# mLSTM gate products on four groups of array columns, partial sums added at the end

## What is computed

```python
xa, za, ub, gb, zb, gates = jnp.split(h @ w_in, ...)
xc = silu(causal_depthwise_conv_3(xa, conv_a_w, conv_a_b))
q = blockdiag(xc, wq)                  # 256 blocks of 4 x 4
k = blockdiag(xc, wk)
v = blockdiag(xa, wv)
gif = concatenate([q, k, v], axis=-1) @ w_if + b_if      # 8 outputs for each position
ig, lf = gif[..., :4], log_sigmoid(gif[..., 4:])
ha = mlstm_chunkwise(q, k * dh ** -0.5, v, ig, lf)
```

## Time and profile before

| what | value |
|---|---|
| median of 3 runs | 3956.01 us |
| lowest, highest | 3952.72, 3957.66 us |
| span of the profiled execution | 3958.0 us |
| PE busy | 3700.5 us, 93% |
| DVE busy | 2176.2 us, 55% |
| POOL busy | 1150.1 us, 29% |
| ACT busy | 901.6 us, 23% |
| mean granted TensorE clock | 0.964 |
| L1295 (`gif`) | 64 records, 30.2 us busy, between 2734.5 and 2884.4 us |

### The profile page before, as it was taken

How to read it: one execution, slowest core, us unless ns; L and a number is a source line. 1 busy time by engine, 2 the same in 40 slices (tenths; PEclk the granted TensorE clock), 3 DMA queues, 4 the chain that set the end, 5 groups by cost and what they waited for, 6 DMA issues and landing times.

```text
span 3958.0 us, 44173 instructions
## 1 busy us (share of the span) xinstructions
PE 3700.5 (93%) x17330; PEld 3000.4 (76%) x17330; DVE 2176.2 (55%) x2115; ACT 901.6 (23%) x1003; POOL 1150.1 (29%) x505
## 2 busy tenths in 40 slices
PE   7778999998999999998999999998999799998997
PEld 5667878877787887776788888876678688877875
DVE  7698451275744663444421221254369988866646
ACT  3344121121122332201210000022322122224221
POOL 0000434333333222223343443442122111214432
PEclk9999999999999999999999999998999899999998
DMA  3234313352135654543111111123333455563421
GB/s 128 72 81 118 98 46 114 109 154 64 32 124 147 157 151 121 153 104 106 43 48 48 48 48 48 40 88 91 130 123 128 141 148 173 145 205 128 156 85 59
DMA packets 538866, 415.58 MB, mean 105 GB/s; under 512 B 33352, under 2 KB 496584, under 8 KB 538720
## 3 DMA queue, kind: packets, MB, share of 16 engines
q1 hardware_dynamic: 477168, 293.94, 26.9%
q10 hardware_dynamic: 61552, 119.65, 8.1%
HBM read 291.00 MB, written 120.16 MB: 104 GB/s over the span
## 4 chain that ended last, share of the span: by engine, by line
PE 76%; DVE 15%; DVEq 3%; ACT 2%; issue 2%; DMA 1%; SPq 0%; ACTq 0%; POOL 0%; POOLq 0%
PE proj_ps L444 65%; DVE WORK L1112 5%; DVE Hlo L591 1%; ACT stage L472 1%; PE mix_ps L1295 1%; PE mix_ps L2160 1%; PE mix_ps L2159 1%; DVE Hlo L593 1%; PE mix_ps L695 1%; DVEq L551 1%; PE mix_ps L1442 1%; DVE AUX L674 1%; PE proj_ps L1453 1%; DVE WORK L2560 0%; PE mix_ps L701 0%
## 5 line engine op out<-in xcount | busy, mean ns | idle before, releaser
L444 PE MATMUL proj_ps<-Hhi,w_hi 128*128 128x512 f32 x4144 | 1330.9, 403 | 110.7 <-DVE Hlo L591 58.9
L444 PE MATMUL proj_ps<-Hlo,w_hi 128*128 128x512 f32 x4144 | 1293.6, 394 | 0.0
L444 PE MATMUL proj_ps<-Hhi,w_lo 128*128 128x512 f32 x4144 | 1289.5, 393 | 0.0
L411 POOL TENSOR_TENSOR w_hi<-w_raw,zero_col 128x1024 fp32r<-128x1024 f32 (+2 forms) x225 | 429.1, 1907 | 2165.3 <-PE proj_ps L444 1662.1
L444 PEld LDWEIGHTS proj_ps<-Hhi,w_hi 128*128 128x128 f32 x4144 | 774.9, 191 | 309.5 <-issue 84.5
L444 PEld LDWEIGHTS proj_ps<-Hlo,w_hi 128*128 128x128 f32 x4144 | 787.7, 190 | 169.0
L444 PEld LDWEIGHTS proj_ps<-Hhi,w_lo 128*128 128x128 f32 x4144 | 786.8, 190 | 168.8
L414 POOL TENSOR_TENSOR w_lo<-w_raw,w_hi 128x1024 fp32r<-128x1024 f32 (+2 forms) x225 | 583.5, 2593 | 32.0
L1112 DVE SCALAR_TENSOR_TENSOR WORK<-WORK,param_cols 128x1024 f32<-128x1024 f32 x240 | 368.3, 1535 | 18.8
L401 POOL TENSOR_TENSOR w_lo<-w_raw,w_hi 128x1024 fp32r<-128x1024 f32 x48 | 135.4, 2820 | 559.4 <-ACT w_hi L395 559.4
L472 ACT ACTIVATE stage<-proj_ps 128x1024 f32<-128x1024 f32 x112 | 130.2, 1163 | 634.8 <-PE proj_ps L444 633.9
(11 more groups left out here) (421 smaller groups left out, 3614.7 us busy)
## 6 DMA issues: line engine op xcount, KB each, us to landing
w_raw<-in_w_in SPq DMA_DIRECT2D x101, 512.0 KB, 4.7
w_raw<-in_sgu_w_in SPq DMA_DIRECT2D x24, 512.0 KB, 3.8
w_raw<-in_w_out SPq DMA_DIRECT2D x24, 512.0 KB, 4.1
w_raw<-in_w_gate SPq DMA_DIRECT2D x22, 512.0 KB, 3.8
w_raw<-in_w_up SPq DMA_DIRECT2D x22, 512.0 KB, 3.8
w_raw<-in_s_w_in SPq DMA_DIRECT2D x16, 512.0 KB, 4.4
WORK<-mid_acs SPq DMA_DIRECT2D x8, 1024.0 KB, 16.7
mid_qkv<-stage ACTq DMA_DIRECT2D x16, 512.0 KB, 5.3
```

Source lines behind the costliest of these rows:

```text
L411: nc.gpsimd.tensor_tensor(whi[slot][:, 0:kt, :], w, zero_col[:, 0:1].unsqueeze(2).to_broadcast([P, kt, P]), ALU.add)
L444: mm = nc.tensor.matmul(ps[:, h * HALF:(h + 1) * HALF], a[slot][:, k, :], b[:, at + k, h * HALF:(h + 1) * HALF], start=(k == 0 and n == 0) ...
```

## The change

`GIF` becomes four outputs of 512 columns in one bank, on the partitions 0, 32, 64 and 96 and the seven above each: xc and xa, each for its two halves of the positions. `gif` is called once in a round, behind part 2, and issues the four products one behind the other; before, the two for xc stood behind part 1. Each group accumulates over the eight rounds by itself (start at k = 0, stop at k = 7). At the end ACT copies the four outputs out in four reads of 512 columns, xc's into `mp_g`, xa's into `mp_lf`, and DVE adds the two and the bias in one instruction, which now increments `gif_ready`.

```diff
-        GIF = PS[0:2 * ML_HEADS, SEQ:2 * SEQ]
+        GIF = [PS[32 * g:32 * g + 2 * ML_HEADS, SEQ:SEQ + HALF] for g in range(4)]
...
+            dve.wait_ge(S("gif_parts"), 1)
+            nc.vector.scalar_tensor_tensor(out=mp_g[0:8, :], in0=mp_g[0:8, :], scalar=mp_b4[0:8, :], in1=mp_lf[0:8, :],
+                                           op0=ALU.add, op1=ALU.add).then_inc(S("gif_ready"), 1)
             dve.wait_ge(S("xs_stored"), 16 * KT)
...
-                def gif(src, w, start, stop):
-                    for h in range(2):
-                        mm = nc.tensor.matmul(GIF[:, h * HALF:(h + 1) * HALF], w, src[:, h * HALF:(h + 1) * HALF], start=start, stop=stop)
+                def gif():
+                    for m, src in enumerate((xc, xa)):
+                        for h in range(2):
+                            mm = nc.tensor.matmul(GIF[2 * m + h], mp_G[:, 16 * k + 8 * m:16 * k + 8 * m + 8],
+                                                  src[:, h * HALF:(h + 1) * HALF], start=(k == 0), stop=(k == KT - 1))
                     return mm
...
-                gif(xc, mp_G[:, 16 * k:16 * k + 8], k == 0, False)
                 pe.wait_ge(S("mp_qkv_sb"), 3 * k + 1)
...
                 tile(2)
-                gif(xa, mp_G[:, 16 * k + 8:16 * k + 16], False, k == KT - 1).then_inc(S("mp_gif"), 1)
+                gif().then_inc(S("mp_gif"), 1)
                 tile(3)
...
             act.wait_ge(S("mp_gif"), KT)
-            nc.scalar.activation(mp_g[0:8, :], GIF, ACT.Identity, bias=mp_b4[0:8, :]).then_inc(S("gif_ready"), 1)
+            for m, dst in enumerate((mp_g, mp_lf)):
+                for h in range(2):
+                    a = nc.scalar.activation(dst[0:8, h * HALF:(h + 1) * HALF], GIF[2 * m + h], ACT.Copy)
+            a.then_inc(S("gif_parts"), 1)
             ug(1, 2, alone=True)
```

## The result

The changed kernel takes 3930.5 us (median of 4 runs, 3928.0 to 3933.7), the kernel before 3955.8 (4 runs, 3952.7 to 3957.7). The ratio is 0.9936, with a 95% interval of 0.9922 to 0.9950: between 20 and 31 us less, 25.3 by the medians. The forecast was 21.65 us less, 3934.4.

A forecast was written before the change was run, and what follows sets the result against it. PE was taken to bound the eight rounds; seven rounds giving 19.6 us and the last 2.05 made 21.65 us off 3956.0, so 3934.4. The range was 3930 to 3945 (0.84), with 3930 to 3938 for four groups at once.

The forecast's parts named there:

- PE bounds the rounds, and stays the bound: In the eight mLSTM preparation rounds, time off PE comes off the chain; DVE's wait shrinks about 2.8 us a round.
- The first call: xc's gate products behind tile part 1 go from each round: 1.95 us less, taken between 1.81 and 2.01.
- Four groups at once: The second call's eight records run on four column groups together: 0.96 us in place of 1.82; chance 0.62.
- rival of a reading limit: In the second call, four groups stream only as fast as two, so it stays at 1.8 us: 3941.2; chance 0.14.
- the rival of program order: In the second call, records start strictly in program order, five steps, 2.13 us in place of 0.86: 3944.5; chance 0.08.
- the two of no overlap and of draining between groups: In the second call: eight records in a row, 3954.8, chance 0.08; each group change drains the array, 3959.6, chance 0.05.
- The tail: Behind the last round's last call, ACT's reads and DVE's sum: next tile at 5.85 us, 0.1 earlier than before.
- The sum: Whole kernel: seven rounds give 19.6 us and the last round 2.05, together 21.65 less, 3934.4.
- The stretch behind: Sign of being wrong: the part behind the eight rounds is longer than before.
- the rival of time given back later: The DVE-bound stretch behind the rounds gives the saving back, leaving the total within 0.2%; chance 0.03.
- The size of chance: Whole-kernel time: a median of runs moves by 2.5 us, allowed for in the range 3930 to 3938.

The follow-up runs named there:

- the runs with one, two and four groups: A round's four products in one call on one, two or four column groups (four is the change): 3951.9, 3938.7 and 3930.5 us.
- the doubled products: The changed kernel with every round's four products issued twice, first into an unused bank: 3940.3 us in one execution.
- the turned order: The kernel with two column groups, with both products of the first group issued before both of the second: 3933.2 us in one execution.
- the changed kernel's second median: The changed kernel run once more, unaltered: 3931.6 us, ratio 0.9935 to the kernel before.

## Why the prediction was right

- *PE bounds the rounds, and stays the bound.* This held. No piece of another engine entered the chain. DVE's wait for the copy (L1224) went from 81.2 us in seven rounds to 63.9: 2.5 a round less, where 2.8 were expected, and nowhere near zero.

```profile
DVE WORK L1224 <- ACT WORK L1347: 63.9, 7, 10.7
```

- *The first call.* I bounded it by 1.81 and 2.01 and took 1.95. The round lost 2.86 in all, of which the joined call accounts for 0.85 (1.82 to 0.97), so the first call gave back 2.01: its own piece and the full restart of L1309. The upper bound was the right one, and my term was 0.06 a round too small.
- *Four groups at once.* 0.96 forecast, 0.97 measured. The step from L2164's two halves to four quarters held (the prediction takes L2164's call as 0.82 us for the factor and as 0.87 for the rate; either way the factor is about two), and the runs with one, two and four groups show that it is the number of groups that counts. The rival of a reading limit falls with the doubled products, the rival of program order with the turned order, the two of no overlap and of draining between groups with the call itself.
- *The tail.* From the start of the last call: PE in front of the transposes at 4.96 (4.85 forecast) after a wait of 0.96 (0.9), next tile at 5.90 (5.85), ACT's four reads 2.40 (2.4), DVE's sum 1.27 (1.28).
- *The sum.* The stretch lost 22.09 against 21.65 forecast. A round lost 2.86 where the sum had 2.8, which makes 0.42 in seven; this is the 0.06 of the first call (the second gave 0.85 for 0.86, and 2.81 had been rounded to 2.8). The last round lost 2.07 against 2.05: 0.06 more by its first call, 0.05 less by the tail, since the next tile came at 5.90 and not at 5.85.
- *The stretch behind.* I named it a sign of being wrong if this part came out longer than before. In the two profiles it did, by 1.3 us (1068.89 to 1070.22). The kernel before alone moves it by 6.6 us from one execution to the next, so this sign was too sharp to say anything, and the rival of time given back later stays open for a us or two.
- *The size of chance.* This term was too small. The median fell by 25.3, 3 more than the stretch, and came to lie half a us above the lower end of my range; that it stayed inside owes something to luck. I had allowed 2.5 us for the movement of a median. Against the 20 executions of the kernel before in the experiments, the changed kernel's second median lies 23.2 lower, 1.1 from the stretch. In the runs beside the experiments, the kernel before alone went from 3945.3 to 3963.0 in 31 executions, with medians of 3954.7 (20 of them) and 3951.7 (7) in two groups of runs. An example of where such time sits, before against after, in windows between the same instructions of the retention stage, far ahead of the change:

```profile
1520.00:1830.00 310.00, 284.45 (x1472) 225.34 (x1472) 139.68 (x117) 63.14 (x64) 75.77 (x32) 0.95 0.46 128
```

```profile
1517.30:1824.10 306.80, 281.08 (x1472) 222.75 (x1472) 138.91 (x117) 63.14 (x64) 75.71 (x32) 0.97 0.46 129
```

The same 1472 records take 3.2 us less, with a mean granted clock of 0.97 instead of 0.95: in the one execution the clock was at its half level, 1.2 GHz, for longer. Why it stayed there longer was not tried.

On the Trainium skill, "TensorE: Matmul & The Clock Gate", Part 3: its measured 2.38x is for three column tiles, which no kernel here ran, so the runs neither confirm nor refute it. Four gave 3.6x by the calls (3.53 to 0.97) and 4.0x without the leaving, and the 1.4 us that I had worked out from it for the eight records did not come. Its rule that matmuls keep program order in their starts, and that weight loads overlap only across row groups, doesn't hold here: eight weight loads, all on 128 rows, were done in 0.12 us while the first records ran, and the turned order cost nothing (1.83 for 1.82, with two groups).

## What to carry to other kernels

A product with few output rows and a long moving operand can leave room for others beside it: here four of them, each with its own 32 output partitions, took 0.97 us together where one behind the other they took 3.53. When PE is the bound, look for up to four such products that can stand together. It matters more that they are in one call than how they are ordered (with two groups the order made no difference). Each call pays for entering and leaving, about 0.3 us here, and a call that fills only two groups takes as long as one that fills four (0.96 and 0.97). Then look at the reader: partial sums on four groups of partitions need more reads, and these stand on the path once, behind the last call. To see a change of half a percent, cut the trace at the first and the last instruction that it touches; the stretch repeated to 0.01 us (four traces of the kernel before, two of the changed one) where whole executions of one kernel differed by more than 10.

## What was not expected of the hardware

- The rate of the moving operand. Four fp32 products together stream 4.8 columns per ns, twice what any place in the trace before showed.
- Four matmuls writing different 32-partition groups of one PSUM bank do not hold each other up: eight more records, four at a time into one bank, add 0.86 us, two steps of the same 0.43 as with one group.
- What joining gives is not a fixed price: 0.27 us a round with one group, 1.14 with four.
